# The context's SwiGLU in three pieces between other phases, and more phases fed by VectorE's block transposes

## The reference

```python
def swiglu(h, w_gate, w_up, w_down):
    return (jax.nn.silu(h @ w_gate) * (h @ w_up)) @ w_down

x = macaron_ffn(x, mod[:, 0:3], *ffn1)
ctx = macaron_ffn(ctx, mod_ctx[:, 0:3], *ffn1)
h_ctx_f, h_ctx_b = context_states(ctx, mod_ctx[:, 3:6], ...)
x, _, _ = mix_sublayer(x, mod[:, 3:6], h_ctx_f, h_ctx_b, *mix)
x = macaron_ffn(x, mod[:, 6:9], *ffn2)
```

## Time and profile before

| quantity | value |
|---|---|
| median of 3 runs | 1655.94 us (1655.23 to 1656.16) |
| the profiled execution's own time | 1655.53 us |
| its span, first to last instruction | 1653.7 us |
| PE busy | 1644.4 us (99%) |
| DVE busy | 1236.7 us (75%) |
| ACT busy | 929.8 us (56%) |
| POOL busy | 213.6 us (13%) |
| weight slots | 561 of 512 KB |

### The profile page before, as it was taken

How to read it: one execution, slowest core, us unless ns; L and a number is a source line. 1 busy time by engine, 2 the same in 40 slices (tenths; PEclk the granted TensorE clock), 3 DMA queues, 4 the chain that set the end, 5 groups by cost and what they waited for, 6 DMA issues and landing times.

```text
span 1653.7 us, 22989 instructions
## 1 busy us (share of the span) xinstructions
PE 1644.4 (99%) x8784; PEld 1418.7 (86%) x8784; DVE 1236.7 (75%) x1639; ACT 929.8 (56%) x1401; POOL 213.6 (13%) x310
## 2 busy tenths in 40 slices
PE   9999999999999999999999999999999999999998
PEld 7888888888888888888899888888888889988887
DVE  6888776788999777778888776655756569986564
ACT  6655567655565555555467455454554558665543
POOL 1100100004311012121310011000002012310000
PEclk9999999999999999999999999999999999999999
DMA  8977553787878777787755458654667545357551
GB/s 284 345 261 258 169 191 108 239 302 247 273 250 285 272 258 241 257 312 248 249 177 187 158 174 279 195 187 142 225 221 242 197 138 199 114 180 240 187 195 64
DMA packets 102430, 361.64 MB, mean 219 GB/s; under 512 B 12720, under 2 KB 13232, under 8 KB 102320
## 3 DMA queue, kind: packets, MB, share of 16 engines
q1 hardware_dynamic: 92736, 334.73, 60.0%
q0 software_dynamic: 9440, 25.36, 4.8%
q10 hardware_dynamic: 144, 0.07, 0.0%
HBM read 355.85 MB, written 1.12 MB: 216 GB/s over the span
## 4 chain that ended last, share of the span: by engine, by line
PE 93%; DVE 3%; DMA 1%; ACT 1%; issue 1%; DVEq 0%; POOLq 0%; POOL 0%; ACTq 0%
PE dn L607 28%; PE gu L532 15%; PE tp L578 11%; PE gu L578 11%; PE tp L585 6%; PE gu L585 6%; PE dn L547 4%; PE tp L560 2%; PE gu L560 2%; DMA raw<-in_weights 1%; PE tp L565 1%; PE gu L565 1%; PE dn L578 1%; DVE w_lo L1878 1%; PE dn L532 1%
## 5 line engine op out<-in xcount | busy, mean ns | idle before, releaser
L1878 DVE TENSOR_TENSOR w_lo<-raw,w_hi 128x1024 fp32r<-128x1024 f32 x518 | 635.5, 1240 | 287.0 <-ACT w_hi L1227 283.6
L1227 ACT ACTIVATE w_hi<-raw 128x1024 fp32r<-128x1024 f32 x520 | 547.3, 1056 | 432.1 <-PE gu L585 140.3
L532 PE MATMUL gu<-w_hi,hT 128*128 128x512 f32 x832 | 259.6, 393 | 1.1 <-DVE w_lo L1871 0.5
L607 PE MATMUL dn<-w_hi,actT_hi 128*128 128x512 f32 x608 | 237.9, 391 | 0.0
L607 PE MATMUL dn<-w_lo,actT_hi 128*128 128x512 f32 x608 | 236.7, 389 | 0.0
L607 PE MATMUL dn<-w_hi,actT_lo 128*128 128x512 f32 x608 | 236.7, 389 | 0.0
L578 PE MATMUL tp<-hT,w_hi 128*128 128x512 f32 x800 | 198.9, 391 | 0.0
L578 PE MATMUL gu<-hT,w_hi 128*128 128x512 f32 x800 | 189.4, 389 | 0.0
L532 PEld LDWEIGHTS gu<-w_hi,hT 128*128 128x128 f32 x832 | 154.1, 188 | 33.9 <-DVE hT L1886 1.5
L578 PEld LDWEIGHTS gu<-hT,w_hi 128*128 128x128 f32 x800 | 150.2, 188 | 31.2
L578 PEld LDWEIGHTS tp<-hT,w_hi 128*128 128x128 f32 x800 | 147.0, 188 | 28.4
(11 more groups left out here) (368 smaller groups left out, 2111.4 us busy)
## 6 DMA issues: line engine op xcount, KB each, us to landing
raw<-in_weights SPq DMA_DIRECT2D x561, 512.0 KB, 4.3
arena<-in_ada_w SPq DMA_DIRECT2D x72, 512.0 KB, 4.4
post_row<-in_post_rows POOLq DMA_DIRECT2D x10, 512.0 KB, 5.3
pre_row<-in_pre_rows POOLq DMA_DIRECT2D x10, 512.0 KB, 7.0
mod_row<-mod POOLq DMA_DIRECT2D x9, 512.0 KB, 9.4
arena<-xn POOLq DMA_DIRECT2D x96, 32.0 KB, 4.3
shift_row<-mod POOLq DMA_DIRECT2D x5, 512.0 KB, 9.0
x<-in_x_in SPq DMA_DIRECT2D x4, 256.0 KB, 5.8
```

What stands on the lines that cost most here:

```text
L532: m = pe.matmul(bank, h[:, k, t * P:(t + 1) * P], w[:, r, kk * 512:(kk + 1) * 512], start=k == 0 and q == 0, stop=k == KT - 1 and q == 2)
L607: m = pe.matmul(dn[:, t, c], a[:, k, :], w[:, r, c], start=start and q == 0, stop=stop and q == 2)
L1227: act.activation(o, i, ACT.Copy, **kw).then_inc(done, 1)
L1878: dve.tensor_tensor(w_lo[:, r, :], raw[:, n % RAW, :], w_hi[:, r, :].bitcast(F32), ALU.subtract).then_inc(lo_ready, 1)
```

## The change

The context's FFN, 66 slots in one phase, becomes three: ctx_a (4 steps, 24 slots) behind ffn_1, ctx_b (3 steps, 18 slots) behind ffn_2, and ctx_c (4 steps, 24 slots) behind sc. ctx_mix moves behind ffn_3. With that the order is ffn_0, ab, ffn_1, ctx_a, ffn_2, ctx_b, sc, ctx_c, ffn_3, ctx_mix, ffn_4, ssd, ffn_5, and no phase from ctx_a to ffn_4 takes its input from the phase just ahead. So:

- ctx_a, ffn_2, sc, ffn_3 and ctx_mix have their inputs turned by DVE and 32 transfers each; ctx_b and ctx_c reload the context's turned input, which ctx_a's has been stored to device memory (`ctx_kept`, `reload`).
- ffn_3 (all steps) and the first two steps of ffn_4 are now by columns. ffn_4's input alone is still turned by PE, in ctx_mix, where sc's was. sc's first eight slots become two column steps, with PSUM banks in another order (`SC_BANKS`).
- The sums of a piece's down products go to `ctx_sum`: ACT copies them out (ctx_a), DVE adds (ctx_b, ctx_c); square, scaling and residual of the context stand in ffn_3.
- `context_x_tokens(1)`, `context_b_tokens`, `context_states` and `x_times` move from sc into the first two steps of ffn_4.
- At sc's end ACT and DVE write the input of ctx_c to `hT`, in the order tile by tile (`FEED`), since the out projection of sc still reads parts of it; PE turns nothing there.
- A column step that waits for halves of its input takes half the contraction of its first and third slot ahead of the second half.
- POOL's order is written out by hand; the 72 loads are spread anew.

```diff
-PHASES = [("ffn_0", SLOTS_FFN), ("ab", 28), ("ffn_1", SLOTS_FFN),
-          ("ctx_ffn", SLOTS_FFN), ("ffn_2", SLOTS_FFN), ("ctx_mix", 11), ("sc", 32), ("ffn_3", SLOTS_FFN),
-          ("ffn_4", SLOTS_FFN), ("ssd", 31), ("ffn_5", SLOTS_FFN)]
+PHASES = [("ffn_0", SLOTS_FFN), ("ab", 28), ("ffn_1", SLOTS_FFN), ("ctx_a", 6 * PIECE_STEPS[0]),
+          ("ffn_2", SLOTS_FFN), ("ctx_b", 6 * PIECE_STEPS[1]), ("sc", 32), ("ctx_c", 6 * PIECE_STEPS[2]), ("ffn_3", SLOTS_FFN),
+          ("ctx_mix", 11), ("ffn_4", SLOTS_FFN), ("ssd", 31), ("ffn_5", SLOTS_FFN)]
...
+EARLY = [s for s in range(PIECE_A, FFN_4 + 1)]
+FED = [s for s in EARLY if s != FFN_4]
+RELOADED = PIECES[1:]
+MOVED = [s for s in FED if s not in RELOADED]
...
-    return s in FFNS and s > 0 and (2 <= j < STEPS - 1 or 0 <= j < 2 and s in APART or j == STEPS - 1 and s + 1 in APART)
+    if s not in FFNS or s == 0:
+        return False
+    last = STEPS_OF[s] - 1
+    return s + 1 in FED if j == last else s in EARLY if 0 <= j < 2 else 2 <= j < last
...
-                for i in range(4):
+                def opened(i, tiles):
                     freed(i)
                     pe.wait_ge(hi_ready, n + i + 1)
-                    upper_products(i, range(KT) if i < 2 else range(1))
+                    upper_products(i, tiles)
+
+                ahead = 1
+                if half_there is None:
+                    opened(0, range(KT))
+                else:
+                    ahead = KT // 2
+                    half_there(0)
+                    opened(0, range(ahead))
+                    opened(2, range(ahead))
+                    half_there(1)
+                    upper_products(0, range(ahead, KT))
+                opened(1, range(KT))
+                between()
...
+                def context_x(j):
+                    if s == FFN_4 and j == 0:
+                        context_x_tokens(1)
+                    if s == FFN_4 and j == 1:
+                        context_states()
...
+                        column_step(n, [column_bank(si) for si in range(4)], bank_freed,
+                                    None if j else lambda half: half_input_there(s, half), lambda: context_x(j))
+                    if s == FFN_4 and j == 0:
+                        context_b_tokens()
...
+                for q in range(0, 3 * KT, 4):
+                    column_step(n0 + q, [sc_bank(p) for p in range(q, q + 4)], lambda i: bank_freed(q + i),
+                                None if q else lambda half: half_input_there(s, half))
...
+            def sums_copied(s, t):
+                for half in range(2):
...
+                    copy(ctx_sum[:, t, half_of(half)], dn[:, t, half_of(half)], dn_copied)
...
                         if by_column(s, j - 1):
                             column_upper(j - 1)
                         elif j:
                             act_upper(j - 1)
+                        if s == FFN_4 and j < 2:
+                            (context_x_tokens, context_b_tokens)[j]()
...
+                def gap_work(j):
...
+                    if s == FFN_4 and j == 0:
+                        dve.wait_ge(tok_ready, TT)
+                        x_times(exp_p)
...
-                closing(s)
+                out0 = n0 + 3 * KT
+                for half in range(2):
+                    fed_lower(s + 1, 0, half)
+                after_slots(out0, 2)
+                out_scaled(s, 0)
+                added(s, 0)
+                after_slots(out0 + 2, 4)
+                fed_lower(s + 1, 1, 0)
+                after_slots(out0 + 6, 1)
+                fed_lower(s + 1, 1, 1)
+                after_slots(out0 + 7, 1)
```

More of the change, by code:

```diff
@@ L78 @@
[L78 to L83, removed]
+PIECES = [SUB.index(name) for name in ("ctx_a", "ctx_b", "ctx_c")]
+PIECE_A, PIECE_B, PIECE_C = PIECES
+FFNS = [s for s, name in enumerate(SUB) if "ffn" in name or s in PIECES]
+FFN_1, FFN_2, FFN_3, FFN_4 = [SUB.index(name) for name in ("ffn_1", "ffn_2", "ffn_3", "ffn_4")]
@@ new lines @@
+MAINS = [s for s in range(len(SUB)) if s not in CTX]
+SOURCE = {s: MAINS[MAINS.index(s) - 1] if s in MAINS and s else None for s in range(len(SUB))}
+SOURCE[CTX_MIX] = PIECE_C
+EARLY = [s for s in range(PIECE_A, FFN_4 + 1)]
+FED = [s for s in EARLY if s != FFN_4]
+RELOADED = PIECES[1:]
+MOVED = [s for s in FED if s not in RELOADED]
+FEED = {s: [(half, t) for t in range(TT) for half in range(2)] if s == PIECE_C else [(half, t) for half in range(2) for t in range(TT)]
+        for s in range(len(SUB))}
@@ L1348, in ffn @@
             def ffn(s, n0):
[L1349 removed]
+                end, last = LAST[s] - TAIL, STEPS_OF[s] - 1
                 def act_upper(j):
@@ L2123, in ffn @@
                     dve.wait_ge(c_ready, 1)
-                for j in range(0 if by_column(s, 0) else 2, STEPS if by_column(s, STEPS - 1) else STEPS - 1):
+                for j in range(0 if by_column(s, 0) else 2, last + by_column(s, last)):
                     n = step_slot(s, j)
+                    if s == FFN_4 and j == 0:
+                        dve.wait_ge(p_exp, 1)
+                        then(dve.tensor_tensor(exp_p[:, :, :], exp_p[:, :, :], dt[:, :, :], ALU.mult))
                     if by_column(s, j):
@@ new lines, in _ @@
+            for v in range(2):
+                pool.dma_start(c_row[:, v, :], small["c_rows"][v, :].partition_broadcast(P)).then_inc(c_loaded, 16)
+            main_opened(0, 14)
+            for tile_name, tile in late_tiles.items():
+                pool.dma_start(tile if tile_name in ("gate_bd", "causal") else tile[:], small[tile_name]).then_inc(late_consts, 16)
+            pool.dma_start(ssd_rows[:], small["ssd_rows"][0, :].partition_broadcast(P)).then_inc(late_consts, 16)
+            pool.wait_ge(late_consts, ALL_LATE)
@@ new lines, in _ @@
+            ada_store(2)
+            post_roots(FFN_3)
+            in_scaled(FFN_4)
+            pre_roots(FFN_4)
+            pool.wait_ge(x_new, X_NEW_N[FFN_3])
+            main_opened(FFN_4, 14)
+            pool.wait_ge(slot_used, BASE["ffn_4"] + 30)
+            for tile_name, tile in (("dft_l", dft_l), ("dft_d", dft_d), ("fourier_bd", fourier_bd)):
+                pool.dma_start(tile, small[tile_name]).then_inc(ssd_consts, 16)
+            pool.dma_start(ssd_norm[:], small["ssd_norm"]).then_inc(ssd_consts, 16)
@@ L2795 @@
         "ffn_1": swiglu_slots("ffn_1", ffn2_w_gate[0], ffn2_w_up[0], ffn2_w_down[0]),
-        "ctx_ffn": swiglu_slots("ctx_ffn", *first),
+        "ctx_a": swiglu_slots("ctx_a", *first),
+        "ctx_b": swiglu_slots("ctx_b", *first),
+        "ctx_c": swiglu_slots("ctx_c", *first),
         "ffn_2": swiglu_slots("ffn_2", ffn1_w_gate[1], ffn1_w_up[1], ffn1_w_down[1]),
```

544 lines of the change are left out of this document (305 added, 239 removed).

## The result

| kernel | median, us | against before |
|---|---|---|
| before | 1655.98 (22 runs) | |
| with the change | 1657.71 (22 runs) | 1.0012, 95% interval 1.0006 to 1.0017 |

The change makes the kernel slower by 0.12%, 1.7 us by the medians and 2.0 by the ratio, where the forecast was 1.2 us faster. The time lies in the range, and under the 0.2% that the prediction called measurable, but the comparison resolves it, and its sign is the other one. One run of the change took 5841.65 us; the ratio is without it, and the median without it is 1657.70.

A forecast was written before the change was run, and what follows sets the result against it. PE, busy for 99% of the span, was taken as the bound. Savings of 5.85 us against two new waits of 2.1 and 2.6 gave -1.15 us, so 1654.7 us, with an 8 in 10 range of 1650.0 to 1660.0.

The forecast's parts named there:

- (a) to (d): PE time saved: ffn_3 by columns 2.62 us, ffn_4's column opening 1.61, sc's end 0.88, sc's first slot 0.10.
- (a): ffn_3 becomes like ffn_2, all by columns, and takes 2.62 us less.
- rival D: Column openings cost what wide ones do, so the change doesn't do what it says: 1659.0 us, chance 0.03.
- (f): From sc to ctx_c, PE waits for DVE's low half behind four `w_lo`: +2.1 us, ends 0.4 and 3.2.
- (g): In ffn_4's second step, PE waits at `context_states` for ACT's B token copies: +2.6 us, ends 0 and 3.5.
- What I cost at nothing: Block transfers, copies and additions of pieces' sums, store and reloads, sc's new banks and moved loads were taken as free.
- rival B: PE's clock falls after the new waits, 2.5 us for each, two of them 5.0: 1659.7 us, chance 0.11.
- (e): PE's 0.64 us of idle time ahead of sc goes; bound +0.8 if ACT is late and DVE's low halves are awaited.
- Rival A: Both new waits, ahead of ctx_c and of `context_states`, are hidden, leaving -5.85 us: 1650.1 us, chance 0.26.
- Rival C: The short ctx_b starves sc: block transfers twice as long land its second tile 10.9 us late: 1665.6 us, chance 0.05.

The follow-up runs named there:

- no_scaling: On top of `two_orders`, POOL's scaling of ffn_4's input left out with nothing in its place: 1650.27 us, 0.9961 of before.
- scaled_in_gap: On top of `two_orders`, DVE instead of POOL scales ffn_4's input, in its idle time at ctx_mix's start: 1649.53 us, 0.9966 of before.
- two_orders: The change with B tokens copied ahead of activations in ffn_4, and ctx_c's input pieces made between weight slots at sc's end: 1652.20 us, 0.9975 of before.
- pool_both: The change with POOL's scaling of ffn_4's input started only when both token tiles of the residual are written: 1660.77 us, 1.0029 of before.

## Why the prediction was wrong

- **The savings (a) to (d)** held as a sum: 5.21 us forecast, some 5.2 in the ledger; ffn_3's 182.28 us shows (a) alone, and with it that column openings don't cost what wide ones do, as rival D had it.
- **(f) and (g)** held: 2.1 forecast, 1.97 and 0.1 of idle time; 2.6 forecast, 2.2. The change's rows show the two queues as worked out: the four weight slots end and the low half follows, and the B copies start behind the activations.

```profile
863.71 4.62 DVE L1952 TENSOR_TENSOR w_lo<-raw,w_hi 128x1024 fp32r<-128x1024 f32 x4
868.25 0.68 DVE L1960 TENSOR_TENSOR hT<-arena,hT 128x512 fp32r<-128x512 f32 x1
```
```profile
1171.10 0.63 ACT L1261 ACTIVATE actT_hi<-act_tok 128x512 fp32r<-128x512 f32 x1 [3.27 <-DVE act_tok L2152]
1171.64 1.07 ACT L1261 ACTIVATE arena<-dn 128x512 f32<-128x512 f32 x2
```

- **The step that failed is "What I cost at nothing"**: its list leaves out one thing that the change adds. sc's input has no modulation, ffn_4's has, and ffn_4 took sc's place behind ctx_mix. So two scalings of 2.4 us came to POOL beside DVE's residual, in a phase where DVE's queue has no gap behind its first weight slot. Price: 1.37 us of PE's idle time ahead of the dt transposes, and what is taken away there reappears ahead of ffn_4 until POOL's scaling leaves the phase (`no_scaling` and `scaled_in_gap` against `two_orders`: 1.9 and 2.7 us by the medians, 2.3 and 1.5 by the ratios to before, whose intervals overlap; ctx_mix itself 34.27 and 34.19 us against 35.89). In before, with nothing of POOL's beside it, the residual took 1.28 us and no wait stood there. The sum has a second cost at nothing, the clock's, which the prediction priced under rival B alone.
- **(e)** was half right: the 0.64 us shrank to 0.15 ahead of ffn_4, only because the phase had lost 1.4 us earlier; its bound, DVE's low halves, I had named, but took for one instruction and not for the end of a full queue.
- **Rival B**, given 0.11, happens in part of the executions: behind the two new waits the clock does fall, at 1.6 us a time where the prediction had 2.5. The forecast's missing 3.0 us are then 1.5 from ctx_mix, some 0.2 from (e), and a rest of 1.3 near the clock's. The clock's is an estimate: falls behind 6 of 14 such waits, at 1.6 us each, make 1.4 us for the two.
- **Rival A**'s price was right, its condition false: nothing hid the two waits, until they were reordered and the scaling moved.
- **Rival C** did not occur: no wait ahead of sc in any profile. I read the Trainium skill's page "SBUF — State Buffer" for POOL's transfers only. The same section, "Who interferes with whom", says that an instruction of VectorE with two inputs in SBUF contends with one of GpSimd that reads SBUF, and that the order of issue decides which is held up. The trace agrees, and that is the missing term: POOL starts first in both pairs of rows above, the residual ends 1125.53 - 1124.45 = 1.08 us behind POOL's scaling, the weight slot 1131.12 - 1130.03 = 1.09 behind the second one, close to the 1.28 and 1.22 that they take alone, as if each had begun when POOL was done.

## What to carry to other kernels

When a phase changes its neighbours, list what each engine now does for the new neighbour, helper engines too, and look whose instructions run beside it: two scalings on a POOL that was busy for 16% of the time cost a quarter of the saving. A wait that is removed in a phase where a second engine's queue is full comes back at the phase's end; it goes for good only when work leaves that queue or moves into its idle time. When a chain moves, hand over its results in the order of need: copying what PE waits for ahead of what it does not removed 4.8 us of waits here and cost nothing. Before a slower median is put down to a queue, hold the granted clock and the phase's own length beside it: of the 3 us that `pool_both` lost, 0.4 were the queue's.

## What the runs showed of the hardware

POOL's elementwise instructions on 128x1024 (2.4 us) held up DVE's with two inputs until they were done, from 1.28 to 2.92 us and from 1.22 to 3.44, while the 160 transfers that POOL issues brought no wait ahead of the phases they feed. After 2 us of idle time the granted clock stayed at 1.00 in some executions and fell to about 0.7 over 6 us in others, behind waits of the same length at the same place; behind two waits of 1.46 us it fell to 0.72 and 0.50. In both kernels with extra matmuls ahead of ctx_c a weight transfer landed some 2 us later, as those matmuls began; nothing here explains it.
